# Joint weight tiles that end one after another, the first projection's rounding on ScalarE, and two groups of transfers issued later, in a two-layer GLA / Mamba-2 / mLSTM trunk

## The reference, cut to what matters

```
for layer in range(2):
    mx, mc = modulation vectors: silu(c) @ w_mod[layer] + b_mod, silu(c_ctx) @ w_mod[layer] + b_mod
    hx, hc = modulate(rmsnorm(x)), modulate(rmsnorm(ctx))
    layer 0: p = h @ a_w_in          # the first 16 column tiles are q, k, v: "the first projection"
             fx, fc = GLA heads and Mamba-2 (SSD) heads over p;  w_o = a_w_out
    layer 1: p = h @ b_w_up
             fx, fc = bidirectional mLSTM with 4x4 block-diagonal wq, wk, wv and gates w_if, b_if;  w_o = b_w_down
    x   = x + mx[2] * (fx @ w_o)
    x   = x + mx[5] * swiglu(modulate(rmsnorm(x)), ffn_w1, ffn_w3, ffn_w2)
    layer 0 does the same to ctx with mc
return rmsnorm(x, final_norm)
```

## Time and profile before

| | us |
|---|---|
| median of 3 runs | 2427.15 |
| lowest, highest | 2422.75, 2593.52 |
| profiled execution, own time | 2426.19 |
| its span, first to last instruction | 2424.5 |
| TensorE busy | 2308.9 (95%) |
| VectorE busy | 1402.4 (58%) |
| ScalarE busy | 885.7 (37%) |
| GpSimd busy | 1043.5 (43%) |
| mean granted TensorE clock | 0.976 |

### The profile page before, as it was taken

The page is one execution under the profiler, slowest core; times in us unless marked ns, Lnnn a source line. Parts: engine busy times, 40 slices in busy tenths (PEclk is TensorE's granted clock), DMA queues, the critical chain, the costliest instruction groups (busy, mean ns, idle before and its releaser), DMA issues.

```text
span 2424.5 us, 32675 instructions
## 1 busy us (share of the span) xinstructions
PE 2308.9 (95%) x11883; PEld 1837.2 (76%) x11883; DVE 1402.4 (58%) x1779; ACT 885.7 (37%) x1919; POOL 1043.5 (43%) x815
## 2 busy tenths in 40 slices
PE   6998999999888999999999999999999989999998
PEld 4887888887535888888888887876555557888886
DVE  4997688665677347757766456542567654111113
ACT  4103435433684156746646352232221212201002
POOL 3453243234542434534444434353122125766664
PEclk9999999999988999999999999999999999999999
DMA  8862342354541244434544223454133212333332
GB/s 266 274 184 89 103 129 84 119 181 144 171 121 30 70 69 132 141 110 121 139 116 126 71 76 118 130 165 138 58 110 98 65 44 70 108 94 99 96 97 81
DMA packets 392723, 281.06 MB, mean 116 GB/s; under 512 B 33442, under 2 KB 357820, under 8 KB 392604
## 3 DMA queue, kind: packets, MB, share of 16 engines
q1 hardware_dynamic: 333420, 200.46, 28.8%
q10 hardware_dynamic: 59184, 78.99, 9.6%
HBM read 237.34 MB, written 42.07 MB: 115 GB/s over the span
## 4 chain that ended last, share of the span: by engine, by line
PE 60%; DVE 5%; ACT 2%; issue 1%; ACTq 1%; DMA 1%; POOL 0%; SPq 0%; DVEq 0%; POOLq 0%
PE PS L928 43%; PE PS L1435 4%; PE PS L1606 3%; PE PS L1447 3%; PE PS L1558 2%; PE PS L1526 1%; ACT nh L1711 1%; PE PS L869 1%; PE PS L1507 1%; DVE xcr L2434 1%; ACTq L2102 1%; PE PS L863 0%; PE PS L1384 0%; PE PS L1318 0%; ACT fprod L2053 0%
## 5 line engine op out<-in xcount | busy, mean ns | idle before, releaser
L928 PE MATMUL PS<-act_hi,w_hi 128*128 128x512 f32 (+1 forms) x1824 | 646.0, 354 | 19.6 <-POOL w_lo L738 4.8
L735 POOL TENSOR_TENSOR w_hi<-w_raw,ones 128x128 fp32r<-128x128 f32 x244 | 134.4, 551 | 1210.6 <-DMA w_raw<-in_ffn_w 429.1
L928 PE MATMUL PS<-act_lo,w_hi 128*128 128x512 f32 (+1 forms) x1824 | 637.9, 351 | 0.0
L928 PE MATMUL PS<-act_hi,w_lo 128*128 128x512 f32 (+1 forms) x1824 | 635.3, 348 | 0.0
L738 POOL TENSOR_TENSOR w_lo<-w_raw,w_hi 128x1024 fp32r<-128x1024 f32 (+1 forms) x244 | 588.9, 2414 | 20.3
L928 PEld LDWEIGHTS PS<-act_hi,w_hi 128*128 128x128 f32 x1824 | 347.5, 190 | 77.9 <-issue 14.9
L928 PEld LDWEIGHTS PS<-act_hi,w_lo 128*128 128x128 f32 x1824 | 345.7, 190 | 47.3
L928 PEld LDWEIGHTS PS<-act_lo,w_hi 128*128 128x128 f32 x1824 | 346.8, 190 | 45.5 <-issue 1.2
L2053 ACT ACTIVATE fprod<-mf_ring,cs 128x128 f32<-128x128 f32 x896 | 267.9, 389 | 27.5 <-DVE mf_acc L2349 27.5
L2349 DVE TENSOR_REDUCE mf_acc<-fprod 128x128 f32<-128x1024 f32 x112 | 225.1, 2021 | 89.9 <-ACT fprod L2053 89.9
L736 POOL TENSOR_SCALAR w_hi<-w_raw 128x896 fp32r<-128x896 f32 (+1 forms) x244 | 247.1, 1013 | 0.0
(11 more groups left out here) (364 smaller groups left out, 3588.2 us busy)
## 6 DMA issues: line engine op xcount, KB each, us to landing
w_raw<-in_ffn_w SPq DMA_DIRECT2D x120, 512.0 KB, 4.1
mf_ring<-in_w_mod SPq DMA_DIRECT2D x56, 512.0 KB, 4.0
w_raw<-in_a_w_in SPq DMA_DIRECT2D x44, 512.0 KB, 4.2
proj<-stage ACTq DMA_DIRECT2D x44, 384.0 KB, 3.9
w_raw<-in_b_w_up SPq DMA_DIRECT2D x32, 512.0 KB, 4.7
m_ring<-in_w_mod SPq DMA_DIRECT2D x12, 1024.0 KB, 7.5
rows<-g_d SPq DMA_DIRECT2D x16, 768.0 KB
m_raw<-in_w_mod SPq DMA_DIRECT2D x4, 2048.0 KB, 12.2
```

The costliest lines, as they stand in the source:

```text
L735: pool.tensor_tensor(w_hi[:, s, 0], w_raw[:, s, 0], ones[:], ALU.mult)
L928: last = pe.matmul(to[:, c0:c1], w[:, s, k, :], x[:, k, c0:c1], start=k == 0 and w is w_hi and x is hi, stop=k == kt - 1 and w is w_lo)
```

## The change

- In `project` and in the mout1 loop, the joint tiles are made together only up to the third last row block; the last two are made tile by tile, and each tile reports its end (mm_done) by itself.
- In "qkv", tiles 4 to 15 are rounded to w_hi by ScalarE (`round_weights`, one instruction over all 8 row blocks, waiting for the load); GpSimd only subtracts. ScalarE does it between its stage copies: tile n+3 behind the copy of tile n. Tiles 0 to 3 stay as they were.
- The spill of x is issued behind the load of tile 10 in place of tile 5.
- The 13 small mLSTM loads are issued behind `hidden(0, T)` in place of ahead of it.

```diff
--- before.py
+++ after.py
@@ -616,7 +616,7 @@
                         load_columns(n)
                     for n in range(RING, 4 * RING):
                         load(n // RING, n % RING)
-                        if n == RING + 1:
+                        if n == 2 * RING + 2:
                             sp.wait_ge(x_put, 12)
                             sp.dma_start(xT_d.rearrange("k p t -> p k t"), xT[:]).then_inc(x_sp, 16)
                         if n + 2 < 4 * RING:
@@ -739,6 +739,14 @@
                                    ALU.subtract).then_inc(w_split, 1)
 
             for name, (n0, count, kt, src) in segs.items():
+                if name == "qkv":
+                    for n in range(RING):
+                        split(0, n, kt)
+                    for n in range(RING, count):
+                        r, s = n // RING, n % RING
+                        pool.wait_ge(w_hi_done, n + 1)
+                        pool.tensor_tensor(w_lo[:, s], w_raw[:, s], w_hi[:, s].bitcast(F32), ALU.subtract).then_inc(w_split, 1)
+                    continue
                 if name == "mix":
                     pool.wait_ge(act_ready, READY["mix0"] + KD)
 
@@ -894,15 +902,18 @@
                         pe.wait_ge(ready, ready0 + 1)
                         for s in range(together):
                             tile_products(s, 0, kt, hi, lo, n, None, ((w_hi, lo),))
-                    for k in range(1 if ready is act_ready else 0, kt):
+                    for k in range(1 if ready is act_ready else 0, kt - 2):
                         pe.wait_ge(ready, ready0 + k + 1)
                         for s in range(together):
-                            last = tile_products(s, k, kt, hi, lo, n)
+                            tile_products(s, k, kt, hi, lo, n)
                             if late and s == 0 and k == 2:
                                 pe.wait_ge(evac, n0)
                                 late_columns(*late)
-                            if k == kt - 1:
-                                last.then_inc(mm_done, 1)
+                    for s in range(together):
+                        for k in (kt - 2, kt - 1):
+                            pe.wait_ge(ready, ready0 + k + 1)
+                            last = tile_products(s, k, kt, hi, lo, n)
+                        last.then_inc(mm_done, 1)
                     for s in range(together, RING):
                         if late and s == 3:
                             pe.wait_ge(m_put, 2 if name == "down00" else 3)
@@ -1629,12 +1640,15 @@
             for s in range(3):
                 pe.wait_ge(w_split, n0 + s + 1)
             pe.wait_ge(evac, n0)
-            for k in range(KD):
+            for k in range(KD - 2):
                 pe.wait_ge(act_ready, READY["ml1"] + k + 1)
                 for s in range(3):
+                    head_products(bank(2 * s), s, k, 2 + k // 4, k % 4)
+            for s in range(3):
+                for k in (KD - 2, KD - 1):
+                    pe.wait_ge(act_ready, READY["ml1"] + k + 1)
                     last = head_products(bank(2 * s), s, k, 2 + k // 4, k % 4)
-                    if k == KD - 1:
-                        last.then_inc(mm_done, 1)
+                last.then_inc(mm_done, 1)
             for m in range(3, KD):
                 pe.wait_ge(w_split, n0 + m + 1)
                 pe.wait_ge(evac, n0 + m - RING + 1)
@@ -1741,7 +1755,17 @@
                 act.wait_ge(evac, r * RING + (s + 1))
                 act.dma_start(proj0[bass.ds(r * RING + (s + tile0), 1)].rearrange("a p t -> p (a t)"), stage[:, s]).then_inc(st_out[s], 16)
 
-            each_ring(act, segs["qkv"][0], 16, lambda r, s: to_stage(r, s, ACT.Copy, 0))
+            def round_weights(n):
+                act.wait_ge(w_in[n % RING], 16 * (n // RING + 1))
+                act.wait_ge(mm_done, n - RING + 1)
+                if n == RING:
+                    act.wait_ge(w_split, RING)
+                act.activation(w_hi[:, n % RING], w_raw[:, n % RING], ACT.Copy).then_inc(w_hi_done, 1)
+
+            for n in range(16):
+                to_stage(n // RING, n % RING, ACT.Copy, 0)
+                if 1 <= n < 13:
+                    round_weights(n + 3)
 
             def load_gate_weights(h):
                 for d in range(2):
@@ -2095,6 +2119,7 @@
 
             norm("ffn0", T, 0, 1)
             act.wait_ge(act_ready, READY["ffn0"] + KD)
+            hidden(0, T)
             for m, w in enumerate(("b_wq", "b_wk", "b_wv")):
                 act.dma_start(w4[:, m], a[w][0].rearrange("n d e -> (n d) e").rearrange("(t p) e -> p t e", p=P)).then_inc(wb_in, 16)
             for d in range(2):
@@ -2103,7 +2128,6 @@
             for d in range(2):
                 for k in range(2):
                     act.dma_start(bif[4 * d:4 * d + 4, k:k + 1], a["b_b_if"][0, d, 4 * k:4 * k + 4].unsqueeze(1)).then_inc(wb_in, 16)
-            hidden(0, T)
             norm("mix1", T, 1, 0, permute=True)
 
             def block_copies(t):
```

## The result

| us | before | changed |
|---|---|---|
| median | 2425.65 (4 runs) | 2398.71 (4 runs) |
| lowest, highest | 2422.75, 2593.52 | 2396.32, 2402.26 |
| profiled execution, its span | 2426.19, 2424.5 | 2399.49, 2397.8 |
| mean granted clock | 0.976 | 0.983 |

A forecast was written before the change was run, and what follows sets the result against it. TensorE, busy 2308.9 us, was taken as the bound, with 115 us of standing still and low clock behind pauses changeable. Terms -11.2 - 5.5 - 2.7 = -19.4 on 2426.2 gave 2406.8, forecast 2408 as median; range 2397 to 2421.

The forecast's parts named there:

- Spill: First projection: moved behind tile 10, TensorE's tiles end 4.8 us earlier and VectorE's blocks 4.0 us earlier.
- the bound chosen (0): Cost of the spill at its new place, taken as 0; upper bound 4.0 us on VectorE's chain, 4.8 on TensorE's.
- Rounding: First projection: moving it to ScalarE gives VectorE 7.2 us over 12 splits, bounds nothing and 21.2 us.
- Rival 2: First projection: the port blocks for whole instructions, VectorE gains 21.2 and 4.0 us; 2403 us, chance 0.12.
- front: First projection up to the gates: 11.2 us less, bounds 4 and 16 us.
- below 187: Sign in the changed kernel's profile: VectorE's last reduction in the first projection ending before 187 us would point to rival 2.
- the case forecast: Whole kernel: 2408 us, chance 0.6, with VectorE's last reduction ending near 190.5 and the gates near 196.
- TensorE's own arrival: At the first gates: TensorE would be there at 193.3 us, leaving a wait of 2.9 us for VectorE.
- Loads: Layer-0 feed-forward: 13 small loads moved behind it remove a 3.9 us wait and 1.6 us of low clock, -5.5 us.
- Joint tiles: mout1 and up10: first tile ends 1.38 us earlier, waits shrink from 1.7 to 0.3 us, -2.7 us together.
- Rival 3: Joint-tile groups: the wait for the last row blocks takes over, slower than before, 2435 us; chance 0.04.
- rival 4: Low-clock stretches fall elsewhere, as in SSD, 1.6 to 3.1 us each; widens every case by some 4 us; no chance given.

The follow-up runs named there:

- the kernel with the long fillers: The changed kernel with 20, 26, 24 and 26 products of ones added in four pauses of TensorE; 2406.31 us (5 runs), ratio 0.9907.
- mid-block experiment: The changed kernel with GpSimd's subtraction, from tile 9 on, waiting until VectorE has done 6 multiply-adds of a block; 2395.15 us (one run).

## Why the prediction was right in its range and 9 us too high

**Spill: right in mechanism, and right in size on the mean.** No wait on tile 6, none on m_ring, nothing late at the new place, as the bound chosen (0) said. VectorE's 4.0 us came as 3.3 over the profiles, and as 0.65 in the first of them.

One execution of the changed kernel does show a wait of 1.1 us for m_ring, and the kernel with the long fillers, the same program up to there, one of 3.6; both come at 83 to 86 us, ahead of the spill's new place, so they aren't its doing.

**Rounding: this is the step that failed**, "I take two thirds, 0.6 x 12 = 7.2 us". With the spill's 4.0 it put VectorE's last block 11.2 us earlier, and a wait of 2.9 us ahead of the gates; measured are 26.5 us, and no wait. As the price of the rounding alone 7.2 was nearly exact. I went through VectorE's operations in the 12 blocks and put what each took beyond its undisturbed pace (0.40 for a multiply-add, 0.26 for a scaled copy) down to the GpSimd instruction beside it:

| us lost by VectorE to | before | changed |
|---|---|---|
| roundings (w_hi) | 9.2 | 1.8 |
| subtractions (w_lo) | 34.1, in 16 | 18.9, in 14 |
| rd's split | 2.9 | 3.0 |
| DMA | 4.1 | 0 |

The roundings gave back 7.4 us. Another 15.2 are in the instruction that was kept. Two fewer fell in the 12 blocks because these end earlier, 4.3 us; the other 11 us are a matter of place. Before, near the end of a block, it was the roundings that ran beside transpose and reduction, and the subtraction behind them met the scaled copy in full. The kernel before, one such place, GpSimd and then VectorE:

```profile
190.67 0.94 POOL L736 TENSOR_SCALAR w_hi<-w_raw 128x896 fp32r<-128x896 f32 x1
191.69 2.40 POOL L738 TENSOR_TENSOR w_lo<-w_raw,w_hi 128x1024 fp32r<-128x1024 f32 x1
```

```profile
191.87 2.37 DVE L2328 TENSOR_SCALAR m_acc<-m_ring,cs 128x256 f32<-128x256 f32 x1
```

I had noted that some roundings were covered by a reduction and took a third off for it. I did not ask what moves under the cover when they leave. In the changed kernel blocks 6, 7, 9, 10 and 11 last 8.3 us and TensorE's tiles 8.4, so the subtraction meets the same place again and again, for 0.58 us instead of 2.14. Two more profiles of the kernel come to nearly the same total of the 12 blocks (116.6 and 117.5 us for 116.3) with their blocks otherwise divided. The mid-block experiment takes just this away and costs 8.6 us on VectorE's chain, with all roundings gone as before.

**Rival 2 had the right front by the wrong road.** By the prediction's own sign, a last reduction "below 187", the case forecast was refuted and rival 2 held. It put VectorE's last block at 201.75 - 25.2 = 176.5, the gates on TensorE's own arrival and the front at -16; measured 175.3 to 176.8, unheld gates, and -16.7 with the clock. But its price, 1.77 us a split, is not what a rounding cost: 0.21 + 0.68 = 0.9 where both fall on multiply-adds, each its own length less 0.4, the one operation that VectorE completes beside it. On the lock the traces bear the Trainium skill out better than I used it. Its page SBUF — State Buffer, section "SBUF: two separate sides", names as parties of the lock only VectorE operations with two SBUF inputs or in a two-port mode. Multiply-adds and scaled copies are stretched here to the GpSimd instruction's length (2.64 beside 2.53, 2.37 beside 2.40), and transposes (0.71) and reductions (0.69) never are. No view here shows whether a scaled copy runs in such a mode.

**TensorE's own arrival** was put at 193.3; the gates came at 192.0 to 193.4. That bound is why 25.7 us on VectorE became 14.6, and why a better rounding would give nothing more: the mid-block kernel loses 8.6 us on VectorE and its gates come at 193.3 all the same. Front: -16.7 against the forecast -11.2. Of it -1.5 was there before, so the change made -15.2.

**Loads: right.** -5.7 and, alone, -5.5; forecast -5.5. The squares start 5.0 us late on the changed kernel's clock (1351.3 + 22.8 = 1374.1 against 1369.07), forecast 1375.7, and catch up in two tiles.

**Joint tiles: right.** -2.8, alone -2.9; forecast -2.7, from 1.7 to 0.3 in both places. Rival 3 did not come: waits on L2409's act_lo were 2.5 us in two before and are 1.7 in three now.

**Low clock elsewhere (rival 4)** was given 4 us either way; -1.5, -4.6, +5.2 and -1.6 make -2.5 in this profile. With the other 4.0 of the front and 0.4 by which GLA and SSD end lower, that is 6.9 of the 7.3 us between -19.4 and -26.7. The last 2 us between 2408 and 2398.7 are the medians, which lay 1 us above the profiled execution before and 0.8 below it after. The measured 2398.7 lies only 1.7 us inside the range, at the end that came from rival 2 and the 4 us of this one. The forecast case itself had missed it by 9, so the range caught it through rival 2 and not by the working of the forecast.

What stays open: why GpSimd's instruction holds VectorE from its next multiply-add on in some places (137.54) and in others not before the transpose (146.87, 3.45 us long, with two multiply-adds behind its start at their usual pace). The same section of the Trainium skill says that whichever starts first has the pair for the whole instruction, which the first place bears out and the second doesn't. Open is also how much of the spill's 4 us by the medians survives more runs.

## What to carry to other kernels

When two engines share a port, price an instruction by what it meets and not by its length, and when one of a chain goes away, ask where the ones behind it now fall. Work out the second-latest arrival first: it caps whatever the latest can give. A pause of 3 us can cost half as much again in the clock behind it, and filler matmuls slightly shorter than the pause recovered some of that here; compare several profiles before calling a stretch of low clock gained or lost.

## What the runs showed of the hardware that was not expected

- Where a GpSimd instruction holds VectorE among its multiply-adds, VectorE completes one operation beside it, whatever the length: 0.64, 1.12 and 2.44 us cost 0.21, 0.68 and 2.14.
- GpSimd is held too: a rounding of 0.46 us took 2.28 when begun at 188.41, about 2 us before a transpose (kernel before), and a subtraction of 2.4 took 3.45 at 146.87 (changed kernel).

```profile
188.41 2.28 POOL L735 TENSOR_TENSOR w_hi<-w_raw,ones 128x128 fp32r<-128x128 f32 x1 [4.12 <-DMA w_raw<-in_a_w_in]
```

- A product of `ones` (128x128, float32) takes 0.23 us and stands in the trace as two matmuls.
- The same program had the low clock behind a 2.6 us pause in one profile and not in two others, which came from other runs; two of the three are known to be of different chips.
